# Where a broadcast write, a block of constants and twenty-seven small loads are issued, an earlier split of weights in four FFNs, and an attention mask added by TensorE

## The chip, the cores and the metric

One core of a Trainium2 chip runs the whole program. The metric is the device time of one execution in microseconds. TensorE (PE), VectorE (DVE), ScalarE (ACT), GpSimd (POOL) and SyncE (SP) run their own instruction streams and wait for each other by semaphores. DMAs are issued from two queues here, SP's (q1 in the trace) and ACT's (q10).

## The reference, cut to what matters

A model in float32 over 256 tokens of width 1024: first two layers, each FFN, mixer, FFN with modulation from `silu(c) @ ada_w`, then four layers, each mixer, cross attention to a memory, FFN.

```python
def first_block(...):
    c_act = silu(c)
    for l in range(2):
        mod = c_act @ ada_w[l] + ada_b[l]                  # nine vectors of 1024
        x = x + 0.5 * gt1 * swiglu(modulate(rmsnorm(x), sh1, sc1), ffn1_w_in[l], ffn1_w_out[l])
        # mixer: 8 heads of causal attention (here), a gated convolution, gated linear attention
        s = where(k_pos <= q_pos, q @ k.T * scale, -1e30); p = softmax(s)
        x = x + gt2 * mixed @ mix_w_out[l]
        x = x + 0.5 * gt3 * swiglu(modulate(rmsnorm(x), sh3, sc3), ffn2_w_in[l], ffn2_w_out[l])
def second_block(...):
    mem_n = rmsnorm(mem)
    for i in range(4):
        x = x + mixer_i(rmsnorm(x))          # i = 0 and 3: diff_attention, with rel_bias[:, bucket(q - k)]
        x = x + cross_attention(rmsnorm(x), mem_n)
        x = x + swiglu(rmsnorm(x), w_gu[i], w_down[i])
    return rmsnorm(x)
```

## The kernel before

**Weights.** Every weight matrix is cut into units of 128x2048 float32 (1 MB; 0.5 MB for an FFN's second matrix). SP streams them in one fixed order into four slots of `raw`; unit n of a slot may be loaded when unit n-1 has been split. ACT rounds a unit to `whi` (L710), DVE subtracts to get `wlo` (L1068), and PE multiplies hi by hi, hi by lo and lo by hi. `ahead(pos)` in ACT's and DVE's streams says where in the order of their work the next units are split: up to three units ahead, but no unit whose slot was last filled at or after `pos`. Splitting a unit waits until PE has used the slot's last one (`used`).

**FFN.** It has 11 steps. Step j multiplies the slots A and B (gate and up, `ab` or `ab_wide`), ACT and DVE form silu(a)*b, and `outs` multiplies it by the 0.5 MB units of the slots O0 and O1, while A and B of the next step have gone before. The order on PE is A0, B0, A1, B1, outs(0), A2, B2, outs(1), and so on. There are eight FFNs. The first four belong to the first block (`st.i` 0 to 3; the first also computes modulation in steps 0 to 9: two or four 1 MB units of `ada_w` a step, multiplied on DVE in `ada_pair`, L1169 and L1172). The last four are "deferred": PE starts on x times the gain while the norm's sum of squares is still under way, and the root is multiplied in afterwards (`st.defer`, L1262 to L1278). `rstd` is made by ACT at L769 and L771 after PE's sum (L1824), which PE does between A0 and B0.

**Start.** SP issues the first constants, the first rows, the memory, four units of `ada_w`, the tokens, and then `ada_w` and FFN units, the rest of the constants (0.83 MB) and the gate weights. ACT begins with 27 small loads (rows, convolution weights, bucket table, positions, lambdas), and then does silu of c and copies the transposed memory. PE transposes the rows and the memory, waits for all small loads (`rows_in`, `misc_in`), transposes them, and only then does the memory's norm sum (L1828), the bias line (a 33x384 product), the reductions of `ada_pair`, the tokens' transposes and two units of `ada_w` directly (L1771, 64 matmuls); then the norm of the first FFN.

**Bias rows.** DVE copies the bias line (8 heads x 384) into `raw` (slot 3), and SP writes it 128 times into a scratch tensor in HBM: 8 partitions, 1024 rows of 1536 bytes, 1.5 MB. The first use of slot 3 for weights waits for that write. The scratch tensor is read by the first `diff` stage, after the fourth FFN.

**Mixer of the first block.** Eight heads run in a loop of steps j (L1505 to L1541 on DVE, L1994 to L2029 on PE), interleaved with nine levels of the linear attention. In step j, DVE first updates the operands of level j (L1399, L1400), masks and takes the maxima of head j (L1514 to L1517), scales the probabilities of head j-1 (L1524, L1525) and keeps the level's blocks (L1424); PE does the scores of head j (L2002, L2003), transposes head j-2, multiplies the values of head j-3, and does level j (L1956), which waits for DVE's update.

Of the kernel before, what the change touches and what calls it, by code (L numbers as in the profile page):

```python
# [28 lines left out]
P = 128  # L29
D = 1024  # L30
KT = D // P
S = 256
# [175 lines left out]
def build(nc, a, out):  # L208

    ctx = ExitStack()  # L210
    with ctx:
# [69 lines left out]
        bias_line = raw[:, 3, 1408:1792]  # L281
# [112 lines left out]
        for l in range(DEPTH1):  # L394
# [12 lines left out]
                                masked=take("masked", 8), pairs=take("pairs", 4), tree=take("tree"),  # L407
# [181 lines left out]
        def _(sp):  # L589
# [34 lines left out]
            for st in stages:  # L624
                if st.kind == "prologue":
# [13 lines left out]
                    stream(1)  # L639
                    for u in range(6, 8):  # L640
                        ada(u)
                    stream(2)
                    load(q["const_rest"], con[:, N_FIRST:], c[:, N_FIRST:N_RESIDENT])
                    sp.wait_ge(q["pro_s"], 1)
                    load(q["const_rest"], gate_w[112:128, :, :], a["gla_gate_w"].rearrange("l r c -> r l c"))

                    sp.wait_ge(*PRO.at(0, "line"))
                    load(q["bias_out"], scratch.rearrange("r h c -> h r c"),
                         bias_line[0:8, :].rearrange("h (o c) -> h o c", o=1).broadcast_to([8, P, 384]))
                elif st.kind == "ffn":  # L650
                    stream(st.pos + 2)
                    if st.ada:
# [5 lines left out]
                        for j in range(STEPS - 1):  # L658
# [3 lines left out]
                            u += per[j]  # L662
                    stream(st.pos + 2 + 4 * (STEPS - 1) + 2)
# [38 lines left out]
        def _(act):  # L702
# [11 lines left out]
            def prologue(st):  # L714

# [13 lines left out]

                act.wait_ge(*PRO.at(0, "vec"))  # L730
                f(silu_c[:, :], col("c", 0, KT), ACT.Silu).then_inc(q["c_ready"], 1)
                for p in range(4):
                    act.wait_ge(q["tok_turned"], p + 1)
                    f(mem[:, 2 * p:2 * p + 2, :], ps[:, 4 + p, :], ACT.Copy).then_inc(q["tok_copied"], 1)
# [15 lines left out]
            def norm(st):  # L750
# [37 lines left out]
            def ffn(st):  # L788
                A, B, _, O1 = st.slots
                lo0 = STEPS * st.i  # L790
                for j in range(STEPS):
# [90 lines left out]
            def mix1(st):  # L882
# [174 lines left out]
        def _(dve):  # L1057
# [36 lines left out]
            def bias_and_lambda():  # L1094
                dve.wait_ge(q["misc_turned"], 2)
                pro("line", v.tensor_copy(bias_line[0:8, :], ps[0:8, 0, 0:384]))
# [6 lines left out]
            def prologue(st):  # L1103
                first_columns(st)
                other_columns(st)
# [1095 lines left out]
```

## Time and profile before

| | |
|---|---|
| three runs | 3074.69, 3080.16 and 3080.6 us; median 3080.16 |
| profiled execution | 3077.22 us, of which the span of the trace is 3075.4 us |
| mean granted TensorE clock | 0.960 of full |
| PE, PEld, DVE, ACT busy | 2855.6, 2694.5, 1956.7, 1370.3 us |
| chain that ended last | PE 81%, DVE 10%, ACT 3%, issue 3%, DMA 2% |
| HBM read, written | 528.10 MB, 2.62 MB |

Times in the trace count from the span's start. A busy PE is not PE at its peak: at the lower of its two clocks (0.50 in the rows, 1.2 GHz, against 1.00, 2.4 GHz) it is busy and half as fast. So both its idle time and the clock beside it have to be read.

### The profile page before, as it was taken

The numbers are of one execution on the slowest core, as the hardware profiler recorded it, in microseconds if no ns is written. First come the engines' busy times: TensorE is split into PE (matmuls) and PEld (weight loads), VectorE is DVE, ScalarE is ACT, GpSimd is POOL, SyncE is SP. The second block draws the span as 40 slices with busy tenths as digits, with TensorE's granted clock in tenths as the row PEclk, the third lists the DMA queues.
The fourth block names the chain that finished last, engine by engine and source line by source line (L and its number), as shares of the span: only waits on it lengthen the run. The fifth ranks groups of instructions, "written<-read, shape, count | busy, mean of one in ns | idle before, by whom it ended". The sixth has DMA issues, their size and how long they took to land.

```text
span 3075.4 us, 50735 instructions
## 1 busy us (share of the span) xinstructions
PE 2855.6 (93%) x21031; PEld 2694.5 (88%) x21031; DVE 1956.7 (64%) x2718; ACT 1370.3 (45%) x1640; POOL 0.7 (0%) x5
## 2 busy tenths in 40 slices
PE   6999879999998899969999978999989999979998
PEld 5999869999996899959899967989989899959897
DVE  5887767778768554555466674556655656555665
ACT  3335444343352444544444514454544544444443
POOL 0000000000000000000000000000000000000000
PEclk8999999999997999979999999999999999979999
DMA  8987418969852255615255613345654456513443
GB/s 239 317 276 243 136 42 280 299 217 301 294 161 82 79 193 187 212 55 165 94 191 181 205 55 111 123 165 181 202 165 137 140 188 204 193 51 128 158 171 109
DMA packets 458799, 533.02 MB, mean 173 GB/s; under 512 B 9879, under 2 KB 435081, under 8 KB 458633
## 3 DMA queue, kind: packets, MB, share of 16 engines
q1 hardware_dynamic: 457340, 530.11, 52.4%
q8 instruction: 109, 1.79, 0.2%
q10 hardware_dynamic: 1293, 0.65, 0.1%
q14 instruction: 57, 0.47, 0.0%
HBM read 528.10 MB, written 2.62 MB: 173 GB/s over the span
## 4 chain that ended last, share of the span: by engine, by line
PE 81%; DVE 10%; ACT 3%; issue 3%; DMA 2%; SPq 0%; ACTq 0%; DVEq 0%
PE ps L1887 14%; PE ps L1720 12%; PE ps L1872 11%; PE ps L2166 8%; PE ps L1873 5%; PE ps L1702 5%; PE ps L1704 5%; PE ps L1703 5%; PE ps L1750 2%; PE ps L1749 2%; PE ps L1748 2%; PE ps L1956 2%; DMA work<-in_ada_w 2%; PE ps L1927 2%; DVE work L1445 1%
## 5 line engine op out<-in xcount | busy, mean ns | idle before, releaser
L1068 DVE TENSOR_TENSOR wlo<-raw,whi 128x2048 fp32r<-128x2048 f32 (+1 forms) x514 | 977.1, 1920 | 475.2 <-ACT whi L710 474.9
L710 ACT ACTIVATE whi<-raw 128x2048 fp32r<-128x2048 f32 (+1 forms) x514 | 824.9, 1611 | 407.0 <-PE ps L1704 115.6
L1872 PE MATMUL ps<-parts_f,whi 128*128 128x512 f32 x1408 | 506.4, 403 | 9.0 <-issue 9.0
L1702 PE MATMUL ps<-hhi,whi 128*128 128x256 f32 x1360 | 390.3, 287 | 12.6 <-issue 10.0
L1873 PE MATMUL ps<-parts_f,wlo 128*128 128x256 f32 x1408 | 398.3, 283 | 0.0
L1703 PE MATMUL ps<-hlo,whi 128*128 128x256 f32 x1360 | 387.3, 285 | 0.0
L1704 PE MATMUL ps<-hhi,wlo 128*128 128x256 f32 x1360 | 387.3, 285 | 0.0
L1887 PE MATMUL ps<-ghi,whi 128*128 128x256 f32 x1280 | 362.4, 283 | 4.0 <-DVE wlo L1068 4.0
L1887 PE MATMUL ps<-glo,whi 128*128 128x256 f32 x1280 | 362.2, 283 | 0.0
L1887 PE MATMUL ps<-ghi,wlo 128*128 128x256 f32 x1280 | 362.1, 283 | 0.0
L1872 PEld LDWEIGHTS ps<-parts_f,whi 128*128 128x128 f32 x1408 | 267.7, 190 | 74.9 <-issue 10.2
L1702 PEld LDWEIGHTS ps<-hhi,whi 128*128 128x128 f32 x1360 | 263.9, 194 | 13.3 <-issue 13.0
L1873 PEld LDWEIGHTS ps<-parts_f,wlo 128*128 128x128 f32 x1408 | 269.1, 191 | 0.1
L1703 PEld LDWEIGHTS ps<-hlo,whi 128*128 128x128 f32 x1360 | 263.8, 194 | 0.0
L1704 PEld LDWEIGHTS ps<-hhi,wlo 128*128 128x128 f32 x1360 | 263.5, 194 | 0.0
L1887 PEld LDWEIGHTS ps<-ghi,whi 128*128 128x128 f32 x1280 | 245.4, 192 | 6.6 <-issue 4.5
L1720 PE MATMUL ps<-hhi,whi 128*128 128x256 f32 x1120 | 231.1, 288 | 17.0 <-DVE hlo L1233 16.2
L1887 PEld LDWEIGHTS ps<-ghi,wlo 128*128 128x128 f32 x1280 | 245.5, 192 | 0.0
L1887 PEld LDWEIGHTS ps<-glo,whi 128*128 128x128 f32 x1280 | 245.4, 192 | 0.0
L1720 PE MATMUL ps<-hhi,wlo 128*128 128x256 f32 x1120 | 227.3, 285 | 0.0
L1720 PE MATMUL ps<-hlo,whi 128*128 128x256 f32 x1120 | 227.2, 285 | 0.0
L1172 DVE SCALAR_TENSOR_TENSOR work<-work,silu_c 128x256 f32<-128x256 f32 x490 | 196.9, 480 | 0.0
(257 smaller groups left out, 4842.4 us busy)
## 6 DMA issues: line engine op xcount, KB each, us to landing
raw<-in_ffn_w_in SPq DMA_DIRECT2D x88, 1024.0 KB, 8.2
raw<-in_ffn_w_gu SPq DMA_DIRECT2D x88, 1024.0 KB, 5.0
work<-in_ada_w SPq DMA_DIRECT2D x72, 1024.0 KB, 8.7
raw<-in_ffn_w_out SPq DMA_DIRECT2D x88, 512.0 KB, 5.8
raw<-in_ffn_w_down SPq DMA_DIRECT2D x88, 512.0 KB, 5.7
raw<-in_ca_w_kv SPq DMA_DIRECT2D x32, 1024.0 KB, 5.8
raw<-in_mix_w_in SPq DMA_DIRECT2D x24, 1024.0 KB, 6.1
raw<-in_da_w_in SPq DMA_DIRECT2D x24, 1024.0 KB, 5.8
```

The lines of the kernel that those rows point to most:

```text
L710: f(whi[:, s, 0:size], raw[:, s, 0:size], ACT.Copy).then_inc(hi_done[s], 1)
L1068: tt(wlo[:, s, 0:size], raw[:, s, 0:size], whi[:, s, 0:size].bitcast(F32), ALU.subtract).then_inc(lo_done[s], 1)
L1172: m = stt(acc, w, silu_c[:, k:k + 1], acc, ALU.mult, ALU.add)
L1702: mm(dst, wh, xh, start=first, stop=False)
L1703: mm(dst, wh, xl, start=False, stop=False)
L1704: return mm(dst, wl, xh, start=False, stop=last)
L1720: o = mm(ps[:, slot, 256 * m:256 * m + 256], w[:, k, P * m:P * m + P], x_[:, k, :], start=k == 0 and i == 0 and m == 0, stop=k == KT - 1 a ...
L1748: mm(dst, xh[:, k, c], th[:, k, :], start=first, stop=False)
L1872: mm(ps[:, banks[m], :], th[:, k, c], parts_f[:, :, k, :], start=k == 0, stop=False)
L1873: o = mm(ps[:, banks[m], 0:S], tl[:, k, c], fhi[:, k, :], start=False, stop=k == KT - 1)
L1887: o = mm(dst, a_, b_[:, t, :], start=first and t == 0 and i == 0 and m % 2 == 0, stop=False, skip_group_check=True)
L2166: o = mm(ps[:, bank, 256 * m:256 * m + 256], w[:, k, P * m:P * m + P], x_[:, k, :], start=k == 0 and i == 0 and m == 0, stop=k == KT - 1 a ...
```

## The change

1. The write of the bias rows is issued by ACT in step 0 of the fourth FFN instead of by SP at the start. The line stands in `gate_w`, so that slot 3's first use waits for the transposes alone.
2. SP issues the large rest of the constants and the gate weights in step 5 of the first FFN.
3. ACT issues the 27 small loads in the memory's norm, behind silu of c, the memory's copies and its squares. PE does the memory's norm sum before it waits for them; DVE does `ada_pair(2, 1)` before the columns that they bring; PE's bias product stands behind `ada_pair(2, 1, 3)`.
4. In the deferred FFNs ACT and DVE also call `ahead(st.pos + 1)` in the norm, which splits A1; DVE waits for the root one instruction later.
5. In the first block's mixers PE adds the causal mask to the scores in PSUM (identity times mask, two float32 products a head), DVE takes the maxima from PSUM without a masking add, and ACT takes the exponential from PSUM.

```diff
@@ at the start: the line, slot 3, SP
-        bias_line = raw[:, 3, 1408:1792]
+        bias_line = gate_w[0:8, :, :].rearrange("p a b -> p (a b)")[:, 0:384]
...
-                                     (q["bias_out"], 16))[s])
+                                     (q["misc_turned"], 2))[s])
...
-                    stream(1)
                     for u in range(6, 8):
                         ada(u)
                     stream(2)
-                    load(q["const_rest"], con[:, N_FIRST:], c[:, N_FIRST:N_RESIDENT])
-                    sp.wait_ge(q["pro_s"], 1)
-                    load(q["const_rest"], gate_w[112:128, :, :], a["gla_gate_w"].rearrange("l r c -> r l c"))
-
-                    sp.wait_ge(*PRO.at(0, "line"))
-                    load(q["bias_out"], scratch.rearrange("r h c -> h r c"),
-                         bias_line[0:8, :].rearrange("h (o c) -> h o c", o=1).broadcast_to([8, P, 384]))
@@ SP, first FFN
+                            if (st.i, j) == (0, 5):
+                                c = a["constants"]
+                                load(q["const_rest"], con[:, N_FIRST:], c[:, N_FIRST:N_RESIDENT])
+                                sp.wait_ge(q["pro_s"], 1)
+                                load(q["const_rest"], gate_w[112:128, :, :], a["gla_gate_w"].rearrange("l r c -> r l c"))
@@ ACT, norm: the small loads, moved out of prologue() into small_loads()
                 if st.early or st.defer is not None:
                     ahead(st.pos)
+                if st.defer is not None:
+                    ahead(st.pos + 1)
+                if st.source == "mem":
+                    small_loads()
@@ ACT, ffn
+                    if (st.i, j) == (3, 0):
+                        act.wait_ge(*PRO.at(0, "line"))
+                        nc.scalar.dma_start(scratch.rearrange("r h c -> h r c"),
+                                            bias_line.rearrange("h (o c) -> h o c", o=1).broadcast_to([8, P, 384]))\
+                            .then_inc(q["bias_out"], 16)
@@ ACT, mix1
-                        s = m_s[:, j % 2, :]
-                        exp_rows(J, (s[:, 0:P], s[:, P:384]), (s[:, 0:P], s[:, P:384]), stat[:, j % 2, 0:2],
+                        if J > 1:
+                            act.wait_ge(q["turned_mm"], J - 1)
+                        d, s = ps[:, (4, 0)[j % 2], :], m_s[:, j % 2, :]
+                        exp_rows(J, (d[:, 0:P], d[:, P:384]), (s[:, 0:P], s[:, P:384]), stat[:, j % 2, 0:2],
@@ DVE, prologue
                 first_columns(st)
+                ada_pair(2, 1)
                 other_columns(st)
-                ada_pair(2, 1)
                 bias_and_lambda()
@@ DVE, deferred norm and ffn
                     ahead(st.pos)
+                    ahead(st.pos + 1)
                     return
...
-                        if j == 0:
-                            dve.wait_ge(q["norm_rs"], st.late.i + 1)
...
                         dve.wait_ge(read[A], st.reads[A] + j + 1)
+                        if j == 0:
+                            dve.wait_ge(q["norm_rs"], st.late.i + 1)
                         tt(silu_a, silu_a, root, ALU.mult).then_inc(q["ffn_a"], 1)
@@ DVE, mix1
-                            dve.wait_ge(q["turned_mm"], J - 1)
-                        s = m_s[:, j % 2, :]
-                        tt(s, ps[:, (4, 0)[j % 2], 0:384], causal, ALU.add).then_inc(q["masked"], 1)
-                        dve.wait_ge(q["masked"], st.masked + j + 1)
-                        v.tensor_reduce(stat[:, j % 2, 0:1], s[:, 0:P], AX.X, ALU.max, negate=True)
-                        v.tensor_reduce(stat[:, j % 2, 1:2], s[:, P:384], AX.X, ALU.max, negate=True)\
+                            dve.wait_ge(q["exped"], J - 1)
+                        d = ps[:, (4, 0)[j % 2], :]
+                        v.tensor_reduce(stat[:, j % 2, 0:1], d[:, 0:P], AX.X, ALU.max, negate=True)
+                        v.tensor_reduce(stat[:, j % 2, 1:2], d[:, P:384], AX.X, ALU.max, negate=True)\
@@ PE, prologue and start: the waits for the small loads and the transposes of them come into start()
                 turn_tokens(0, tok_mem)
+
+            def start(st):
                 n_rows = sum(2 if r in ("q_norm", "k_norm", "gla_out_norm") else 1 for r in ROWS) - len(FIRST_ROWS)
                 pe.wait_ge(q["rows_in"], 16 * n_rows)
...
-
-            def start(st):
-                pe.wait_ge(*PRO.at(0, "cols"))
-                mm(ps[0:8, 0, 0:384], bias_cols[0:BUCKETS + 1, :], bucket[0:BUCKETS + 1, :], start=True,
-                   stop=True).then_inc(q["misc_turned"], 1)
                 ada_pair(0, 0, 3)
                 pe.wait_ge(q["token_in"], 16)
                 turn_tokens(1, tok_x)
                 ada_pair(2, 1, 3)
+                pe.wait_ge(*PRO.at(0, "cols"))
+                mm(ps[0:8, 0, 0:384], bias_cols[0:BUCKETS + 1, :], bucket[0:BUCKETS + 1, :], start=True,
+                   stop=True).then_inc(q["misc_turned"], 1)
@@ PE, mix1
-                        mm(d[:, 0:P], mq[rows_, tile, 0:P], mk[rows_, tile, 0:P], start=True, stop=True)
-                        mm(d[:, P:384], mq[rows_, tile, P:S], mk[rows_, tile, :], start=True, stop=True)\
-                            .then_inc(q["scores_mm"], 1)
+                        mm(d[:, 0:P], mq[rows_, tile, 0:P], mk[rows_, tile, 0:P], start=True, stop=False)
+                        mm(d[:, 0:P], ident, causal[:, 0:P], start=False, stop=True)
+                        mm(d[:, P:384], mq[rows_, tile, P:S], mk[rows_, tile, :], start=True, stop=False)
+                        mm(d[:, P:384], ident, causal[:, P:384], start=False, stop=True).then_inc(q["scores_mm"], 1)
```

## Rows read from the trace of the kernel before

**Rows 1.** The page: the chain that ended last, by engine.

```profile
PE 81%; DVE 10%; ACT 3%; issue 3%; DMA 2%; SPq 0%; ACTq 0%; DVEq 0%
```

**Rows 2.** Windows at the start: engines busy, then PEclk, DMA share, GB/s.

```profile
24.00:44.00 20.00, 20.00 (x106) 17.77 (x104) 16.83 (x51) 8.72 (x18) 0.00 (x0) 0.83 1.06 349
...
57.00:68.00 11.00, 8.33 (x55) 8.07 (x54) 5.86 (x10) 5.78 (x8) 0.00 (x0) 0.84 0.46 53
```

**Rows 3.** Timeline of ACT and its queue: start, duration, operation (first and last of 27 small loads).

```profile
0.73 0.42 ACTq L717 DMA_DIRECT2D raw<-in_mix_norm  x1
...
12.74 0.74 ACTq L717 DMA_DIRECT2D work<-in_da_lk  x1
...
18.28 2.19 ACT L762 ACTIVATE work<-raw 128x512 f32<-128x512 f32 x4
```

**Rows 4.** Timeline of PE to the first FFN; in brackets idle before it.

```profile
7.62 3.67 PE L1693 MATMUL ps<-con,raw 128*128 128x128 f32 x16 [3.20 <-DMA raw<-in_mem]
...
23.70 0.64 PE L1693 MATMUL ps<-con,raw 31*128 31x31 f32 x5 [8.62 <-DMA work<-in_da_lk]
24.27 6.68 PE L1828 MATMUL ps<-work,con 128*128 128x256 f32 x16
...
55.47 0.47 PE L1720 MATMUL ps<-hhi,whi 128*128 128x256 f32 x2 [2.15 <-DVE hlo L1233]
```

**Rows 5.** Timelines of SP, ACT and PE around the bias write.

```profile
39.42 0.81 SPq L593 DMA_DIRECT2D bias_rows<-raw  x1
50.28 17.13 SPq L593 DMA_DIRECT2D raw<-in_ffn_w_in  x2
...
76.39 1.91 ACT L710 ACTIVATE whi<-raw 128x2048 fp32r<-128x2048 f32 x1 [12.45 <-DMA raw<-in_ffn_w_in]
...
80.72 0.55 PE L1702 MATMUL ps<-hhi,whi 128*128 128x256 f32 x1 [8.78 <-issue]
```

**Rows 6.** DMA queues in 13:19: packets, MB, share of 16 engines.

```profile
q1 hardware_dynamic: 1329, 1.33, 70.6%
q10 hardware_dynamic: 872, 0.51, 31.9%
```

**Rows 7.** Timelines of ACT and DVE in the fourth FFN, steps 0 to 2.

```profile
1065.65 3.79 ACT L710 ACTIVATE whi<-raw 128x2048 fp32r<-128x2048 f32 x3
...
1087.52 0.60 ACT L807 ACTIVATE work<-ps 128x512 f32<-128x512 f32 x1 [1.30 <-PE ps L1704]
...
1067.58 4.57 DVE L1068 TENSOR_TENSOR wlo<-raw,whi 128x2048 fp32r<-128x2048 f32 x3 [2.50 <-ACT whi L710]
```

**Rows 8.** Waits of PE in 300:700 and 700:1000; timelines of PE (second mixer), DVE (first).

```profile
PE ps L1956 <- DVE work L1400: 8.3, 6, 2.2
...
PE ps L1956 <- DVE work L1400: 4.1, 4, 2.0
...
996.91 0.63 PE L2002 MATMUL ps<-work 64*128 64x128 f32 x2
997.34 1.06 PE L2003 MATMUL ps<-work 64*128 64x256 f32 x2
...
1000.63 2.24 PE L1956 MATMUL ps<-work 64*128 64x128 f32 x16
...
388.70 0.55 DVE L1514 TENSOR_TENSOR work<-ps,con 128x384 f32<-128x384 f32 x1
```

**Rows 9.** Waits of PE; then its timeline and DVE's in the first deferred FFN.

```profile
PE ps L1872 <- issue: 9.0, 4, 2.3
...
1524.30 0.47 PE L1872 MATMUL ps<-parts_f,whi 128*128 128x512 f32 x1 [2.25 <-issue]
...
1521.91 2.29 DVE L1068 TENSOR_TENSOR wlo<-raw,whi 128x2048 fp32r<-128x2048 f32 x1 [2.50 <-ACT whi L710]
```

**Rows 10.** Windows there: columns as in rows 2.

```profile
1510.00:1515.00 5.00, 5.00 (x30) 4.34 (x29) 4.20 (x8) 1.43 (x3) 0.00 (x0) 1.00 0.46 184
1525.00:1528.50 3.50, 3.50 (x14) 2.97 (x13) 1.09 (x2) 2.29 (x2) 0.00 (x0) 0.55 0.88 288
```

More of the change, by code:

```diff
@@ L406, in build @@
             stages.append(Stage(kind="mix1", l=l, units=units, last=units[-1], gn=take("gn", 5), heads=take("heads", 8),
-                                masked=take("masked", 8), pairs=take("pairs", 4), tree=take("tree"),
+                                pairs=take("pairs", 4), tree=take("tree"),
                                 rope=take("rope", 4)))
@@ L714, in prologue, with small_loads @@
             def prologue(st):
+                act.wait_ge(*PRO.at(0, "vec"))
+                f(silu_c[:, :], col("c", 0, KT), ACT.Silu).then_inc(q["c_ready"], 1)
+                for p in range(4):
+                    act.wait_ge(q["tok_turned"], p + 1)
+                    f(mem[:, 2 * p:2 * p + 2, :], ps[:, 4 + p, :], ACT.Copy).then_inc(q["tok_copied"], 1)
+            def small_loads():
                 def load(semaphore, dst, src):
@@ L728, in prologue @@
                          a[name].partition_broadcast(P).rearrange("p a b -> p (a b)"))
[L730 to L734, printed above, removed]
             def rope_tables():
@@ L1095, in bias_and_lambda @@
                 dve.wait_ge(q["misc_turned"], 2)
-                pro("line", v.tensor_copy(bias_line[0:8, :], ps[0:8, 0, 0:384]))
+                pro("line", v.tensor_copy(bias_line, ps[0:8, 0, 0:384]))
                 pro("cols_s", ts(lam[:, 14:16], col("q_norm", 0, 2), 0.125, None, ALU.mult))
@@ L1494, in mix1 @@
                 rope(3)
-                causal = const("causal")
                 gate_ready = 4 * l + 4
@@ L1987, in mix1 @@
                 pe.wait_ge(q["rope_done"], st.rope + 4)
+                causal = const("causal")
                 def part(h):
@@ L1997, in mix1 @@
                         rows_, tile = part(j)
-                        if st.masked + j > 1:
-                            pe.wait_ge(q["masked"], st.masked + j - 1)
+                        if st.heads + j > 1:
+                            pe.wait_ge(q["exped"], st.heads + j - 1)
                         d = ps[:, (4, 0)[j % 2], :]
-                        mm(d[:, 0:P], mq[rows_, tile, 0:P], mk[rows_, tile, 0:P], start=True, stop=True)
-                        mm(d[:, P:384], mq[rows_, tile, P:S], mk[rows_, tile, :], start=True, stop=True)\
-                            .then_inc(q["scores_mm"], 1)
+                        mm(d[:, 0:P], mq[rows_, tile, 0:P], mk[rows_, tile, 0:P], start=True, stop=False)
+                        mm(d[:, 0:P], ident, causal[:, 0:P], start=False, stop=True)
+                        mm(d[:, P:384], mq[rows_, tile, P:S], mk[rows_, tile, :], start=True, stop=False)
+                        mm(d[:, P:384], ident, causal[:, P:384], start=False, stop=True).then_inc(q["scores_mm"], 1)
                     if 2 <= j <= 9:
@@ L2061, in diff @@
                     if j < 8:
-                        pe.wait_ge(q["masked"], st.masked + j - 1)
+                        if st.masked + j > 1:
+                            pe.wait_ge(q["masked"], st.masked + j - 1)
                         for c in range(2):
```

## The prediction

> **What bounds the kernel now.** I read the page first. PE makes up 81% of the chain that ended last and DMA 2% [rows 1], so in most places only PE's time counts; the places where PE stands still or runs at its lower clock are what the change can reach. I then read PE's waits, the timelines of the four stretches that the diff touches, and windows over them.
>
> At the start the DMA engines are full until 44 us (share 1.06, 349 GB/s), then only the bias write is left: share 0.46 and 53 GB/s [rows 2]. PE waits 8.62 us for the last small load, which was issued at 12.74 and is used at 23.70, and the first FFN begins at 55.47 [rows 3, 4]. SP issued the bias write at 39.42. The load of A1, issued at 50.28 on the same queue, lands only at 76.39, and PE stands still 8.78 us before A1's product [rows 5]. In the four deferred FFNs PE waits 9.0 us in all, 2.25 us each, between B0 and A1 [rows 9]. In the two mixers DVE and PE take turns.
>
> **Part 1: small loads behind silu of c.** They take ACT's queue from 0.73 to 13.48, so 12.75 us for 27. Now ACT does silu, the four copies, a table load and four squares first. The memory's transposes end at 7.62 + 3.67 = 11.29; the last copy adds 0.5, the table load 1.28 and the squares 2.2 [rows 3, 4]: the issue starts at 15.3 and ends at 28.05. The last load starts its issue at 27.3. Before, the last one needed 10.9 us from issue to use (12.74 to 23.70); that gives 38.2. From below it lands at once, 28.1. The engines remain full in between, as they were then, so I take 37. After that load PE had 31.8 us of work and waits to the first FFN, of which 6.6 us were the memory's norm sum (L1828), now done ahead [rows 4]. The rest, 25.2 us, is serial as before: DVE's work behind the bias line is in the same order. First FFN: 37 + 25.2 = 62.2, against 55.5. Term: +6.7 us, from -2.2 to +7.9. Silu comes early, and with it the first two `ada_pair`, but nothing on this path waits for them.
>
> **Part 2: the bias write leaves the start.** A1's load has free engines, lands some 5 us after its issue, and PE goes on after B0. The stall of 8.78 us goes [rows 5]. What is late next is DVE's chain of the step (splits of A1, B1, O0, O1 and two `ada_pair`), which begins with A1's split and moves forward as a whole. I take -8.7; from -4 (if the four `ada_w` units, 4 MB at 349 GB/s or 12 us, become the wait) to -11 (with a stretch at the lower clock gained back).
>
> **Part 3: large constants in the first FFN.** 0.83 MB at 349 GB/s are 2.4 us of all engines. At the start they lay behind everything that PE waited for; in step 5 they lie between weights that are due some 10 us later. +0.3, from 0 to +2.4. The same 3 MB of weights and 2 MB of `ada_w` a step hide it.
>
> **Part 4: the bias write in the fourth FFN.** 53 GB/s are 34.5 rows of 1536 bytes a microsecond. The share of 0.46 means that some 8 of 16 engines carry it [rows 2], 128 rows each at 0.232 us. A 1 MB weight unit has 64 rows of 1 KB for each engine, at 349/16 GB/s or 0.047 us each, so 3 us. On ACT's queue the write no longer stands ahead of the weights in one line; but while both queues had work, at 13 to 19 us, their packets passed at similar rates, 1329 and 872 [rows 6]. I read that as turn by turn on each engine. Then a weight unit needs 64 x (0.232 + 0.047) = 17.9 us on the shared engines. The write is issued after `ghi` of step 0, at 1065.7, which by the 0.81 us of that issue [rows 5] also puts ACT's next splits back (B1's is just in time: +0.5). B2's load can start when B1 is split, 1067.58 + 2.2 [rows 7] plus the 0.8; it flows from about 1072.6 and lands at 1090.5. A2's product ends at 1087.5 (ACT's silu follows it [rows 7]); to be ready then, B2 must land 4.2 us earlier (1.9 for hi, 2.3 for lo), at 1083.3. It is 7.2 us late. Behind it 16 rows of O0 and O1 and the next A, of which 28 rows still alternate, land at about 1106; PE, now 7.2 us later, wanted that A at 1102: 4.1 us more. Lower clock after two such stalls: I add 2. Sum +14. From both sides: 0 if weights pass first, +22 if the write's 29.7 us pass first.
>
> The Trainium skill ("DMA: Bandwidth & Descriptors", section Queues, rings and completion order) says that each engine goes round-robin between its rows of queues, a whole packet of about 9 to 17 descriptors at a time. Working with its figures, an estimate, one turn of the write would last 2 to 4 us and B2 land up to that much later, for a sum of about +16 to +18; the records in this trace look finer than that.
>
> **Part 5: A1 split early in the deferred FFNs.** Before, DVE splits A1 from 1521.91 to 1524.1, PE waits 2.25 us for it [rows 9] and then runs at clock 0.55 for 3.5 us, doing 14 matmuls where 6 a microsecond are normal (30 in 5): 3.5 - 14/6 = 1.2 us lost [rows 10]. Now ACT splits A1 when A0's product ends at about 1515.4, before it makes `rstd`; the root comes 0.9 us later, and DVE's lo of A1 ends at 1519.7, before PE ends B0 at 1522.05. Late next is B1: its slot is free at 1522.05, then a copy 0.6, two DVE operations 1.3, `ghi` 0.6, hi 1.9, lo 2.3, with gaps 1528.9; PE, at full clock, would want it at 1527.6: a new wait of 1.3. For each FFN -(2.25 + 1.2 - 1.3) = -2.15, for four -8.6. Bounds: -3.8 (the clock falls again) to -13.8 (no new wait).
>
> **Part 6: mask by PE.** Removed: 16 DVE additions of 0.55 us [rows 8]. Added: 32 float32 products of identity and mask. The scores' 128-column pair takes 0.43 us from start to start at the lower clock [rows 8], the 256-column pair twice that: 1.28 us a head at the lower clock, about 0.65 at the full one. If all of it hid nothing, +20.8 at the lower clock; if PE had slack everywhere and DVE always bound, -8.8. PE waits for DVE before a level, 6 times in the first mixer (8.3 us) and 4 times in the second (4.1 us), up to 2.2 us [rows 8], and there the products fit in. But head 0 stands ahead of level 0, in steps 4 and 6 DVE waits for ACT's `hhi` behind PE's scores and transposes, and in the second mixer level 6 follows PE's own work without a gap [rows 8]. Counting along the chain: first mixer 1.3 (head 0) + 0.7 (level 3) + 2 x 0.65 - 2 x 0.6 (two steps that DVE bounds) = +2.1; second 1.3 + 0.15 + 0.9 + 1.3 + 1.3 + 0.65 - 2 x 0.6 = +4.4. I take +6, range -4 to +12 as most of the bounds can't hold in all steps.
>
> **Sum.** 6.7 - 8.7 + 0.3 + 14 - 8.6 + 6 = +9.7. The profiled execution took 3077.2 us (span 3075.4 and 1.8 around it): 3086.9. The median of the runs shown, 3080.2, is 2.9 higher, but they spread over 6; I forecast 3087.
>
> **Rivals.**
> (a) *The write in the fourth FFN does not hold the weights.* Then part 4 is +0.5 and the sum -3.8: 3073 with the rest as worked out. This is the case that ends on the other side. It decides once B2 lands before 1083.3, so if a 1 MB unit passes in under 10.7 us beside the write. For it: an alternating packet share of 40 to 60 [rows 6] was read with small packets, and DMA there is under half used. Against it: 0.232 us a row is five times a weight row.
> (b) *PE has room for the mask*, because its extra work also lifts its clock: part 6 is -4, sum -0.3, 3077: no change.
> (c) *Small loads land soon after issue* (31): part 1 is +0.7, sum +3.7, 3081: no change.
> (d) *The early split gains little* (-3.8) since the wait only moves to B1: sum +14.5, 3092.
> The early split could also do nothing if A1 were not landed by then, but it was issued before B0's split ended, 15 us ahead.
>
> **How the numbers follow.** Likeliest, 0.42: all terms near what I took, 3087, own range 3079 to 3097. Rival (a) 0.25, (b) 0.10, (c) 0.10, (d) 0.13. About 0.2% or 6.2 us is what a measurement of this kernel can tell from no change. Slower by more: 0.30 of the first, 0.11 of (d), 0.03 of (c), together 0.44. Same: 0.12 + 0.05 of (a) + 0.06 of (b) + 0.07 of (c) + 0.02 of (d) = 0.32. Faster: 0.20 of (a) and 0.04 of (b) = 0.24. The range reaches down to 3068 (rival (a) with a cheaper mask) and up to 3102 (part 4 at its upper bound).
>
> **What the profile after would show.** Part 1: PE's wait for the last small load ends near 37 and the first FFN begins near 62; near 55 it is wrong. Part 2: no wait of PE before A1's product. Part 4: in the fourth FFN DMA share high at low GB/s for some 35 us, and PE waits of 5 us or more before B2's product; none, and (a) holds. Part 5: no wait at L1872 after B0, a shorter one at B1's product, no clock near 0.5 there. Part 6: each mixer loop 2 to 4 us longer. Wrong I would be most easily in part 4, the largest term, and read from the least direct rows.

## The result, and the profile after

The changed kernel takes 3092.64 us (median of 5, 3089.2 to 3094.02), the kernel before 3080.6 on the same chip (5 runs, 3074.69 to 3083.43): ratio 1.0036, interval 1.0024 to 1.0048. It is slower, by 12 us in the medians. The profiled execution of the changed kernel took 3093.57 us with a span of 3091.8, 16.4 more than the span shown of before.

The page of the changed kernel: the chain that ended last, by engine.

```profile
PE 81%; DVE 10%; DMA 3%; ACT 3%; issue 2%; SPq 1%; ACTq 0%; DVEq 0%
```

Against [rows 1], DMA went from 2% to 3%. That is all that a summary shows of it. So I set each matmul of one trace beside the same matmul of the other and read how much later it begins. PE reaches the first FFN 12 us later, but A1's product of that FFN only 2 us later (82.70 against 80.72), and is 5 to 6 behind from 179 to 300 us, 10 at 429, 6 at 1053, 25 at 1100 and 16 at the end. Where the large steps come from is read below. One trace is not exact about the start: the six kernels whose start is the changed kernel's (it, and experiments 1, 2, 3, 7 and 8) reach the first FFN between 63.6 and 68.4 us and A1's product between 79.7 and 84.4, so a step of a few us there says nothing by itself.

**The start.** Timeline of PE to the first FFN.

```profile
13.89 6.43 PE L1835 MATMUL ps<-work,con 128*128 128x256 f32 x16 [2.63 <-ACT work L760]
26.89 0.73 PE L1700 MATMUL ps<-con,raw 104*128 104x104 f32 x3 [6.57 <-DMA raw<-in_ada_b]
36.31 0.65 PE L1700 MATMUL ps<-con,raw 31*128 31x31 f32 x5 [8.69 <-DMA work<-in_da_lk]
...
45.07 13.81 PE L1778 MATMUL ps<-silu_c,work 128*128 128x1 f32 x64
58.74 6.18 PE L1835 MATMUL ps<-work,con 128*128 128x256 f32 x16
...
67.85 0.76 PE L1727 MATMUL ps<-hhi,whi 128*128 128x256 f32 x2 [2.14 <-DVE hlo L1243]
```

ACT's queue in the same stretch (start, duration): first and last small load.

```profile
13.22 0.39 ACTq L721 DMA_DIRECT2D raw<-in_mix_norm  x1
...
25.43 0.74 ACTq L721 DMA_DIRECT2D work<-in_da_lk  x1
```

Windows there: busy time of PE, PEld, DVE, ACT, POOL, then PEclk, DMA share, GB/s.

```profile
20.00:40.00 20.00, 4.74 (x25) 4.11 (x24) 7.26 (x25) 0.89 (x2) 0.00 (x0) 0.57 1.03 319
40.00:60.00 20.00, 20.00 (x88) 18.53 (x87) 13.88 (x38) 10.31 (x18) 0.00 (x0) 0.50 0.18 57
60.00:80.00 20.00, 17.55 (x96) 16.38 (x96) 12.51 (x21) 10.54 (x15) 0.00 (x0) 0.73 0.28 83
```

The last small load is used at 36.31 instead of 23.70 [rows 4]. PE did the memory's norm sum ahead and then has nothing: it stands still for 6.57 and 8.69 us, and from 40 to 60 it is busy without a pause at clock 0.50, the lower of its two levels (1.2 GHz). Busy in full, with half the speed: the busy column alone would have shown nothing wrong. From the last load to the first FFN it took 31.5 us. The wait of 8.78 us for A1 [rows 5] is gone: between 76 and 100 us PE waits 0.3 us in all.

**The fourth FFN.** Timelines of ACT and its queue, DVE, SP and PE.

```profile
1071.24 0.31 ACTq L828 DMA_DIRECT2D bias_rows<-gate_w  x1
...
1076.71 1.91 ACT L707 ACTIVATE whi<-raw 128x2048 fp32r<-128x2048 f32 x1
1105.38 2.86 ACT L707 ACTIVATE whi<-raw 128x2048 fp32r<-128x2048 f32 x2 [26.76 <-DMA raw<-in_ffn_w_in]
...
1107.32 3.43 DVE L1077 TENSOR_TENSOR wlo<-raw,whi 128x2048 fp32r<-128x2048 f32 x2 [24.44 <-ACT whi L707]
...
1077.21 11.11 SPq L593 DMA_DIRECT2D raw<-in_ffn_w_out  x2
1088.40 21.66 SPq L593 DMA_DIRECT2D raw<-in_ffn_w_in  x2
...
1109.72 0.55 PE L1709 MATMUL ps<-hhi,whi 128*128 128x256 f32 x1 [16.11 <-issue]
```

Windows there (columns as above).

```profile
1072.00:1100.00 28.00, 21.61 (x179) 21.31 (x178) 8.06 (x6) 5.97 (x5) 0.00 (x0) 0.96 0.69 141
1100.00:1112.00 12.00, 2.28 (x11) 2.31 (x12) 4.68 (x4) 6.57 (x7) 0.00 (x0) 0.50 0.54 149
```

The DMA queues in three windows, 1076:1082, 1084:1088 and 1098:1104 (packets, MB, share of 16 engines; q10 is ACT's queue with the write, q1 SP's with the weights), and of the first the landing time of the weights issued in it.

```profile
q10 hardware_dynamic: 194, 0.30, 43.8%
q1 hardware_dynamic: 522, 0.53, 28.9%
raw<-in_ffn_w_in SPq DMA_DIRECT2D x1, 1024.0 KB, 29.3
...
q10 hardware_dynamic: 129, 0.20, 43.7%
...
q10 hardware_dynamic: 193, 0.30, 42.0%
q1 hardware_dynamic: 192, 0.20, 9.2%
```

The write's rows pass from 1073 to 1104 at an unvarying 32 a microsecond, whatever the weights do. B2, issued at 1076, first moves its half on the engines that don't carry the write (522 packets by 1082); then no weight packet at all (1084 to 1088); then weight rows and write rows one for one (192 and 193), and B2 lands with the end of the write, 29.3 us after its issue. PE stands still for 16.1 us and goes on at clock 0.50. This one stall is larger than the whole loss.

**The deferred FFNs and the mixers.** Waits of PE in the changed kernel (total, times, longest); then, of 300:1010 alone, the wait before the levels.

```profile
PE ps L1709 <- issue: 16.5, 2, 16.1
PE ps L1894 <- DVE wlo L1077: 6.6, 3, 3.0
PE ps L1879 <- issue: 5.5, 4, 1.4
...
PE ps L1963 <- DVE work L1410: 7.6, 7, 1.3
```

Against [rows 9], L1879 (L1872 before) waits 1.4 us an FFN instead of 2.25; it is now B1's product and not A1's. In the mixers the waits for DVE before a level [rows 8] became fewer and shorter: 7.6 us in 7 waits, longest 1.3, where the kernel before has 13.7 us in 11 over the same stretch, longest 2.2.

### The profile page after: what moved, and what is told of

Read it like the earlier page. It is cut to its first block, busy times and chain, and to the rows that moved or that the text cites. A ratio compares the mean times of both kernels' runs of the same rounds, so it can differ in the third digit from the quotient of the medians.

```text
span 3091.8 us, 50863 instructions
## 1 busy us (share of the span) xinstructions
PE 2869.4 (93%) x21095; PEld 2704.0 (87%) x21095; DVE 1948.5 (63%) x2702; ACT 1368.1 (44%) x1640; POOL 0.7 (0%) x5
## 4 chain that ended last, share of the span: by engine, by line
PE 81%; DVE 10%; DMA 3%; ACT 3%; issue 2%; SPq 1%; ACTq 0%; DVEq 0%
PE ps L1894 14%; PE ps L1727 12%; PE ps L1879 11%; PE ps L2177 8%; PE ps L1880 5%; PE ps L1709 5%; PE ps L1711 5%; PE ps L1710 5%; PE ps L1757 2%; PE ps L1755 2%; PE ps L1756 2%; DMA work<-in_ada_w 2%; PE ps L1963 2%; PE ps L1934 2%; DVE wlo L1077 1%
## 5 line engine op out<-in xcount | busy, mean ns | idle before, releaser
L1879 PE MATMUL ps<-parts_f,whi 128*128 128x512 f32 x1408 | 500.4, 399 | 5.5 <-issue 5.5
L1879 PEld LDWEIGHTS ps<-parts_f,whi 128*128 128x128 f32 x1408 | 264.7, 188 | 70.1 <-issue 6.7
```

Source lines behind the costliest of these rows:

```text
L1879: mm(ps[:, banks[m], :], th[:, k, c], parts_f[:, :, k, :], start=k == 0, stop=False)
```

## The experiments

All were timed beside the kernel before (3080.22, 3080.45 and 3081.42 us in three sets); "later" and "earlier" are again from the same matmul in two traces.

### 1. The bias write in the second mixer

```diff
-                    if (st.i, j) == (3, 0):          # ACT, fourth FFN: the write
...
                 log_exp_tables()
+                if st.l == 1:
+                    act.wait_ge(*PRO.at(0, "line"))
+                    nc.scalar.dma_start(scratch.rearrange("r h c -> h r c"), ...)
                 for j in range(8 + 3):
```

> The changed kernel, but ACT issues the bias write ahead of the second mixer's head loop instead of in step 0 of the fourth FFN. Theory: the write holds the weights of the fourth FFN on the engines it uses, and that costs the 18.4 us by which PE falls back there; the DMA engines are idle in the mixer loop (share 0.00), so the 31 us of the write fit in: 18 us less than the changed kernel, about 3074, 0.2% below the kernel before. Rival: PE falls back in the fourth FFN for another reason (ACT issuing, or the early order of the loads); then it stays near 3092.

3073.74 us (9 runs), ratio 0.9977 (0.9965 to 0.9988): 18.9 less than the changed kernel. A window over the fourth FFN, and from the DMA view of 953:985 the landing of a weight unit that is issued beside the write in the mixer:

```profile
1065.00:1100.00 35.00, 35.00 (x293) 34.91 (x292) 20.07 (x16) 19.45 (x17) 0.00 (x0) 1.00 0.62 211
```

```profile
raw<-in_ffn_w_in SPq DMA_DIRECT2D x1, 1024.0 KB, 27.9
```

PE is busy for all 35 us at clock 1.00. The write still holds a unit of weights for 27.9 us, but in a mixer nobody waits for it. Beside the changed kernel's trace this one is 4.3 us earlier at 1053 us, ahead of the fourth FFN, and 23.0 at 1115: 18.7 us are gained there. So the write in the fourth FFN cost some 19 us, and the place is what made it cost.

The order of the rows is the same here as in the FFN. DMA queues in 964:972 and 974:984 (the write was issued at 952.77, the held unit at 959.05):

```profile
q10 hardware_dynamic: 259, 0.40, 44.2%
...
q10 hardware_dynamic: 311, 0.48, 42.3%
q1 hardware_dynamic: 309, 0.32, 8.9%
```

For 8 us, and 32 rows of the write on each of its engines, not one row of weights passed; then they went one for one. In both places the change came some 17 to 19 us into the write.

### 2 and 3. The write in eight pieces, and in two halves

```diff
-                    if (st.i, j) == (3, 0):
+                    if st.i == 3 and j < 8:          # the halves: j in (0, 4), 64 rows of each head
-                        nc.scalar.dma_start(scratch.rearrange("r h c -> h r c"), ... [8, P, 384]
+                        nc.scalar.dma_start(scratch[16 * j:16 * j + 16].rearrange("r h c -> h r c"), ... [8, 16, 384]
...
```

SP's wait before it reads the scratch tensor counts all the pieces.

> The changed kernel, with the bias write cut into eight DMAs of 16 of the 128 copies, one in each of the steps 0 to 7 of the fourth FFN. Same bytes, same queue, same FFN. Theory (the weights of the engines that the write uses come one row after each row of the write, or not at all while more than about half of a long write is still ahead of them): 16 rows an engine are over in 4 us, less than the 10 us of slack of a unit: no wait of PE, 17 us less than the changed kernel, about 3075. Rival (the 31 us of the write cost PE the same wherever they are spread in the FFN): 16 us of waits in eight pieces, about 3092.

> The changed kernel, with the bias write cut into two DMAs of 64 copies, in the steps 0 and 4 of the fourth FFN. In the changed kernel the weights' rows on the write's engines came from 1090 on only, half way through the write, and from then one for one with it. Theory A (only so much of a DMA stands ready on each engine, and the second half of the write is taken up before the weights behind it): with 64 rows the weights come one for one from the first, B2 lands some 16 us after its issue instead of 29 and PE waits about 4 us a half: 8 us in all, half of now, about 3084. Theory B (the write passes first, the weights after it, whatever its length): each half costs its 15 us less some 13 of slack: 2 to 4 us in all, about 3079.

Eight pieces: 3070.12 us (8 runs), ratio 0.9969 (0.9956 to 0.9983), 22.5 less than the changed kernel. Two halves: 3073.88 (10 runs), ratio 0.9984 (0.9974 to 0.9994). Not all of the 22.5 us belong to the write: beside the changed kernel's trace the eight pieces are 1.8 us earlier at 1053 us and 20.4 at 1115, so 18.6 are gained in the fourth FFN, as in experiment 1, and another 3.9 in two stages far behind it, at about 1820 and 2700 us, which the edit doesn't touch. The halves gain 15.7 in the FFN, 3 less. A window of the eight pieces; then of the halves ACT's wait for B2, and the landing time of the weights issued in 1068:1083.

```profile
1062.00:1200.00 138.00, 138.00 (x1151) 137.91 (x1150) 70.81 (x67) 63.99 (x57) 0.00 (x0) 1.00 0.59 194
```

```profile
1086.56 2.86 ACT L707 ACTIVATE whi<-raw 128x2048 fp32r<-128x2048 f32 x2 [13.36 <-DMA raw<-in_ffn_w_in]
```

```profile
raw<-in_ffn_w_in SPq DMA_DIRECT2D x2, 1024.0 KB, 13.7
```

The same 1.5 MB through the same queue in the same FFN cost PE no wait if they come 4 us at a time: a piece holds a unit for less than the lead that the weights have. A half (some 15 us) holds B2 about until its own end, and PE waits 2.7 us once; the second half costs no wait. So it is the length of one write beside the lead of the loads, not its bytes. In the trace of the halves the weights' rows on the shared engines come at the very end of the write: they followed it, and did not go one for one. That is theory B's picture, though its time (3079) was 5 us too long.

### 4 and 5. The old start, and the loads alone

```diff
             def prologue(st):
+                small_loads()
                 act.wait_ge(*PRO.at(0, "vec"))
...
-                if st.source == "mem":
-                    small_loads()
```

The "old start" also takes back the order of PE and DVE (transposes of the rows in PE's prologue, the bias product first in `start`, `ada_pair(2, 1)` behind `other_columns`); the write stays in the fourth FFN.

> The changed kernel with the small loads first on ACT's queue again and PE's and DVE's order of the start as before; the bias write and the large constants stay where the change put them. Theory: the late small loads cost 12.4 us at the start of the first FFN: 12 us less than the changed kernel, about 3080, and the first FFN begins near 55. Rival: part of the delay comes back inside the first FFN, whose first two steps wait for ada_w units: 5 to 8 us less, about 3086.

> The changed kernel with one thing of the start undone: the 27 small loads stand first on ACT's queue again, while PE's and DVE's new order (the memory's norm sum and the second ada_pair ahead of them) stays. Theory: the small loads' landing alone sets the start, near 24 us instead of 36, and the memory's sum is off that path: the first FFN begins at 50 to 52, 4 us earlier than in the kernel before, and the run takes 16 us less than the changed kernel, about 3076. Rival: the first FFN is then held by the ada_w units (8 MB before its second step), and all beyond the old start (12 us) is lost again: 3080.

Old start: 3078.52 us (10 runs), ratio 0.9999 (0.9990 to 1.0009): 14.1 less than the changed kernel. Loads alone: 3080.92 (10 runs), ratio 1.0004 (0.9995 to 1.0014), 11.7 less. PE in the old start, then with the loads alone:

```profile
23.73 0.65 PE L1699 MATMUL ps<-con,raw 31*128 31x31 f32 x5 [8.71 <-DMA work<-in_da_lk]
...
33.66 10.28 PE L1777 MATMUL ps<-silu_c,work 128*128 128x1 f32 x64
...
52.38 0.48 PE L1726 MATMUL ps<-hhi,whi 128*128 128x256 f32 x2 [2.14 <-DVE hlo L1242]
```

```profile
18.84 5.66 PE L1834 MATMUL ps<-work,con 128*128 128x256 f32 x16 [7.57 <-ACT work L761]
...
32.40 13.24 PE L1777 MATMUL ps<-silu_c,work 128*128 128x1 f32 x64
...
54.41 0.77 PE L1726 MATMUL ps<-hhi,whi 128*128 128x256 f32 x2 [2.14 <-DVE hlo L1242]
```

The old start reaches the first FFN at 52.38, the loads alone at 54.41, the changed kernel at 67.85. I had expected a gain from the memory's norm sum before the small loads; there is none: PE waits 7.57 us for ACT's squares, and then the 64 products take 13.24 us instead of 10.28. The rival's time (3080) was right; that the `ada_w` units are what takes the gain back isn't shown. The two runs reach A1's product 12.0 and 11.5 us before the kernel before did, and the four runs of experiments 9 to 12, with the same old start, 9.6 to 12.9. That is what taking the bias write out of the start is worth at this place; experiment 11 shows that the constants have no part in it. By 300 us 8 to 10 of it are left in all six.

### 6. PE kept busy while it waits

```diff
+                for _ in range(26):                  # 36 more before the wait for misc_in
+                    turn(ps[:, 3, 0:P], ident)
                 pe.wait_ge(q["rows_in"], 16 * n_rows)
```

It adds 62 transposes of the identity whose results nobody reads.

> The changed kernel, where PE also does 26 and 36 transposes of the identity into a free bank while it waits for the small loads. They add work that nobody uses and leave the result as it is. Theory: of the 12.4 us by which the first FFN begins later, 6 come from the lower TensorE clock (0.50 from 27 to 74 us) after PE stood still for 16 us; with PE busy the clock stays up, the work from the last small load to the first FFN takes 25 us instead of 31.5, and the run is 5 to 6 us shorter, about 3087. Rival: the clock falls in the stretch of one-column matmuls whatever PE did before: no change, 3092.

3088.2 us (6 runs), ratio 1.0024 (1.0011 to 1.0037), 4.4 less than the changed kernel. Windows:

```profile
20.00:40.00 20.00, 13.04 (x95) 12.47 (x94) 7.36 (x25) 0.89 (x2) 0.00 (x0) 0.83 1.01 318
40.00:60.00 20.00, 18.80 (x90) 17.31 (x88) 17.26 (x43) 11.65 (x21) 0.00 (x0) 0.66 0.20 65
```

With useless work before the last load (used at 35.91, hardly sooner than 36.31) the clock behind it is 0.66 instead of 0.50, and the first FFN begins at 60.95 instead of 67.85; A1's product at 77.10 instead of 82.70. The other five traces with the new start have clocks of 0.50 to 0.62 there, the first FFN at 63.6 to 68.4 and A1's product at 79.7 to 84.4, so the filler is worth 3 to 7 us by the traces. In the medians it is 4.4 us, with intervals that overlap. So of the 14.1 us of the new start a few, 4 as the best guess, are the clock, and the rest the late loads. The Trainium skill ("TensorE: Matmul & The Clock Gate", section HAM oscillation) tells of the same thing in a loop that waits for its DMAs: the waits throttle PE, and the work behind each of them starts cold. The two traces agree, with 0.50 behind waits of 6.57 and 8.69 us and 0.66 where the filler left 4.6 and 2.4 of them.

### 7. The mask by DVE again

```diff
-                        mm(d[:, 0:P], ident, causal[:, 0:P], start=False, stop=True)
...
+                        tt(s, ps[:, (4, 0)[j % 2], 0:384], const("causal"), ALU.add).then_inc(q["masked"], 1)
```

> The changed kernel with the mask added by DVE again. Between the traces the first mixer lost about 3 us and the second gained about 5. Theory A (extra PE work lifts the clock sooner in the second mixer): undoing it changes the sum by +2 (-1 to +4), about 3094. Theory B (as forecast: +6.5 us along the chain of DVE and PE, and the second mixer's gain is chance of the clock): 4 to 6 us less, about 3087.

3093.96 us (7 runs), ratio 1.0036 (1.0024 to 1.0049): the changed kernel's own ratio. The mask by PE costs nothing measurable here. Waits of PE in 300:1010:

```profile
PE ps L1963 <- DVE work L1408: 10.9, 9, 2.0
...
PE ps L1963 <- DVE work L1398: 5.0, 2, 2.5
```

With the addition on DVE, PE waits 10.9 us before the levels instead of 7.6, and 5.0 more for L1398, of which the changed kernel (there L1400) has 0.7 left. That fits products that lie in time in which PE waited.

### 8. A1 split late again

```diff
-                if st.defer is not None:              # ACT; on DVE the same call
-                    ahead(st.pos + 1)
```

> The changed kernel without the early split of A1 in the four deferred FFNs (DVE's later wait for the root stays). Theory: the wait of 2.25 us before A1 and the stretch at the lower clock come back four times, while the wait of 1.4 us before B1 goes: 12 us more than the changed kernel (-3.0 a FFN between the traces), about 3104. Rival (only the difference of the waits counts, 0.9 us each, the clock being chance): 3 to 4 us more, 3096.

3097.21 us (4 runs), ratio 1.0059 (1.0039 to 1.0080): the early split is worth 4.6 us in the medians, with intervals that overlap. Without it: waits of PE, then windows 1532:1552 and 1816:1826; in the third fence the same windows of the changed kernel.

```profile
PE ps L1876 <- issue: 9.0, 4, 2.3
```

```profile
1532.00:1552.00 20.00, 17.77 (x97) 15.36 (x97) 9.83 (x14) 9.19 (x12) 0.00 (x0) 0.92 0.36 128
1816.00:1826.00 10.00, 6.64 (x57) 6.51 (x58) 8.63 (x18) 0.00 (x0) 0.00 (x0) 1.00 0.00 0
```

```profile
1532.00:1552.00 20.00, 19.13 (x111) 16.50 (x110) 11.81 (x15) 11.49 (x15) 0.00 (x0) 1.00 0.37 128
1816.00:1826.00 10.00, 7.45 (x45) 7.29 (x45) 6.96 (x14) 0.00 (x0) 0.00 (x0) 0.72 0.00 0
```

At the first deferred FFN the clock stays at 1.00, and behind each of the four PE is 2.4 or 2.5 us earlier (within the first for a moment 4.0). That makes 9.8 us, more than the 8.6 forecast. The rival's time (3096) was nearer than the theory's, but its reason, that only the waits differ, isn't: without the early split the clock there is 0.92. They don't all reach the end: the lead of the first is gone by 1825, where the products of the linear attention's levels (L1963; L1960 in the file without the early split) are done at clock 0.72 where the run without the early split has 1.00. The other three leads are kept but for 1.1 us: 3.0, 5.4 and 6.8 us earlier behind the second, third and fourth FFN. Whether the early split is what lowers that clock, experiment 12 can tell.

### 9 to 12. Both repairs, and three parts priced on top

The old start (experiment 4) with the write in eight pieces (experiment 2); then the same with DVE's mask (the diff of 7), with the constants at the end of SP's prologue (below), and without the early split (the diff of 8).

```diff
                     stream(2)
+                    load(q["const_rest"], con[:, N_FIRST:], c[:, N_FIRST:N_RESIDENT])
...
-                            if (st.i, j) == (0, 5):
```

> The two repairs together: the small loads stand first on ACT's queue with the old order of PE and DVE at the start, and the bias write goes out in eight pieces of 16 rows in steps 0 to 7 of the fourth FFN. Theory: the two costs lie in different places and add: the start is worth 14.1 us against the changed kernel (3092.6 to 3078.5), the pieces are worth 22.5 (to 3070.1), so 3056, ratio 0.992; with the clock giving a little back 3054 to 3062. Rival: a gain at the start is given back before the third FFN (PE meets the same weights' loads sooner), as much of it was where the loads alone were moved: 3064 to 3070.

> As the run with both repairs, but DVE adds the mask again and PE multiplies only queries and keys. Prices the mask by PE where no other part of the change disturbs the mixers. As predicted (+6 for the mask by PE): 6 faster than the run with both repairs. By the run that undid the mask alone (3093.96 against 3092.64): the same within 3. Rival, PE has room: 4 slower than the run with both repairs, and it would show in the second mixer.

> As the run with both repairs, but the large constants and the gate's rows are loaded at the end of SP's prologue again, behind the weights of unit 2. In all versions so far PE lost 2 to 4 us between 101 and 376 us against the kernel before, and step 5 of the first FFN lies at 179. Theory: the constants hold the weights behind them there: then this run gains 2 to 3 us, and the loss between 101 and 376 is gone. Rival: the loss is the lead of the start that the weights' loads take back whatever stands between them: no difference within 2 us, and the constants delay no product at the start either.

> As the run with both repairs, but A1 is split late in the deferred FFNs, as before. Prices the early split a second time. As predicted: 8.6 slower than the run with both repairs. As the run that undid it alone measured (3097.2 against 3092.6): 4.6 slower. Rival, the wait only moved to B1: 2 slower or less.

| kernel | us (5 runs each) | ratio, interval |
|---|---|---|
| both repairs | 3062.63 | 0.9943, 0.9929 to 0.9956 |
| and mask by DVE | 3065.05 | 0.9950, 0.9936 to 0.9963 |
| and constants at the start | 3061.17 | 0.9933, 0.9919 to 0.9946 |
| and no early split | 3066.91 | 0.9957, 0.9943 to 0.9970 |

The chain of both repairs, by engine:

```profile
PE 85%; DVE 8%; ACT 3%; issue 2%; DMA 1%; SPq 0%; ACTq 0%; DVEq 0%
```

Both repairs together beat the kernel before by 0.57% (18.8 us) and the changed kernel by 30 us. The sum of the two differences of medians would have been 36.6, so the theory's 3056 was missed, and 3062.63 lies between it and the rival's 3064. But the rival's reason, that something is given back, doesn't show: beside the changed kernel's trace both repairs are 14.1 us earlier at 300 us, 13.9 at 1053 and 32.5 at 1115, so the start's 14 and the write's 18.6 are there in full, and 30.9 at the end. What is missing is mostly the 3.9 by which experiment 2's 22.5 exceed the 18.6 gained at the write, and 1.6 lost between 1200 and 1520.

Window 375:430, in the first mixer, with both repairs, and (second fence) with DVE's mask as well:

```profile
375.00:430.00 55.00, 46.22 (x294) 32.91 (x294) 38.14 (x118) 21.48 (x53) 0.00 (x0) 0.88 0.00 1
```

```profile
375.00:430.00 55.00, 47.02 (x242) 32.24 (x240) 38.49 (x114) 20.48 (x51) 0.00 (x0) 0.65 0.00 1
```

The mask by PE is worth 2.4 us in the medians, with intervals that overlap; in the traces PE is 5.6 us earlier behind the second mixer, of which 2.3 are left at the end. In these runs it goes with a clock of 0.88 instead of 0.65 in the same stretch; the kernel before, with DVE's mask, has 0.81 there, so the clock of a mixer hangs on more than the mask. The constants are worth nothing in either place (1.5 us, overlapping intervals). The loss against the kernel before between 101 and 376 us stays (2.9 us with the constants at the start, 3.2 without) and so does that between 300 and 429 (4.8 and 4.6): they are not its cause.

The early split is worth 4.3 us in the medians, as in experiment 8. The traces tell more. Behind each of the four FFNs the kernel with it gains 2.3 to 2.5 us again. The kernel without it, however, was 2.8 us ahead before the first deferred FFN, 2.3 of them gained between 1115 and 1520 where both kernels do the same. And the products that ran at 0.72 in experiment 8's comparison do so in both kernels here. Window 1785:1795, with and (second line) without the early split:

```profile
1785.00:1795.00 10.00, 7.45 (x44) 7.29 (x44) 6.93 (x14) 0.00 (x0) 0.00 (x0) 0.72 0.00 0
...
1785.00:1795.00 10.00, 7.45 (x44) 7.29 (x44) 6.46 (x12) 0.00 (x0) 0.00 (x0) 0.73 0.00 0
```

So that clock isn't the price of the early split. What sets it is open.

## Why the prediction was right, and where it was not

The forecast of 3087 with a range of 3068 to 3102 and "slower" as the likeliest held: 3092.64. The range's upper end has a slip: part 4 at its bound of 22 instead of 14 makes 3095 of 3087, not 3102; the measured time lies below either. Part by part, what was forecast and what the runs showed:

| part | forecast | measured |
|---|---|---|
| 1 small loads behind silu | +6.7 | +14.1 (experiment 4) |
| 2 bias write leaves the start | -8.7 | -10 to -13 at A1, -8 to -10 at 300 us (traces of experiments 4, 5, 9 to 12) |
| 3 constants | +0.3 | 0 within 2 (experiment 11) |
| 4 bias write in the fourth FFN | +14 | +18.6 and +18.7 (traces of experiments 1, 2 in that FFN) |
| 5 early split | -8.6 | -9.5 and -9.8 at the four FFNs, -4.6 and -4.3 in the medians (experiments 8, 12) |
| 6 mask by PE | +6 | -1.3, -2.4 (experiments 7, 10) |

With -10 for part 2 and the medians for part 5 the measured parts add to 14.1 - 10 + 0 + 18.7 - 4.5 - 1.9 = +16.4, more than the 12 of the medians and as much as between the two traces; to the tenth that is chance, since medians and traces are mixed and no part is known to better than 1 or 2 us. That the forecast of +9.7 came near the 12 was luck in part, because its errors stood on both sides: parts 1, 4 and 5 together were 16 too low, part 6 some 8 too high.

**Part 1**: the mechanism and the first number were right (last load used at 36.31, taken as 37). The term that was mis-sized is "25.2 us, serial as before": it took 31.5, since the 25.2 were read where PE had a clock of 0.83 from 24 to 44 us [rows 2] and it is 0.50 from 40 to 60 here. A serial stretch was carried over with its duration, but behind new idle time. In the other five traces with the new start the stretch took 27.5 to 32.0 us, and 25.0 in experiment 6, where PE was kept busy in the waits. So the idle time is worth 2.5 to 7 us of it, which is most of the 7.4 by which the part was too low.

**Part 2**: no wait before A1 is left, as forecast; the gain at A1 (10 to 13) was about the bound of 11 or above it, of which up to 4 are given back by 300 us.

**Part 4**: the place, the mechanism (the write holds the weights on the 8 shared engines) and rival (a)'s refutation were right. Mis-sized was the term "64 x (0.232 + 0.047) = 17.9 us", turn by turn: it took 29.3 us, and the upper bound named, the write's whole time passing first, was nearly what came. The reading behind it, that queues pass at similar rates in 13:19 [rows 6], was of small packets on ACT's queue (0.51 MB in 872); in the fourth FFN one for one held only behind about 1090 us, the last 14 of the write's 31 us, and in the mixer of experiment 1 from about 972, the last 13 of its 32. The sentence on the Trainium skill's packet-wise round-robin came to +16 to +18 and was nearer than mine, but its rule doesn't show in the packets either: for 8 us, 32 of the write's rows an engine, not one weight packet passed (experiment 1), and then they alternated row by row. The second stall forecast (4.1 us at the next A) didn't come, since the write was over when B2 landed.

**Part 5**: the new wait (1.3 forecast, 1.4 measured, four times) and the removed one with its clock were right for each FFN, and so was the gain: 2.3 to 2.5 us, where 2.15 was forecast. What the forecast lacks is that only half of the four gains shows in the medians. Part of it went at a clock of 0.72 in experiment 8, and in experiment 12 the kernel without the early split had got 2.3 us elsewhere; neither is shown to come from the early split, and with 4 and 5 runs the medians themselves are uncertain by some 3 us.

**Part 6**: counted along the chain in both mixers, it gave +6; rival (b), that PE has room (-4), was nearer. The step that failed is "head 0 stands ahead of level 0, in steps 4 and 6 DVE waits for ACT's `hhi` behind PE's scores", each taken at its full price: PE's waits for DVE before a level fell from 13.7 to 7.6 us over both mixers. The mixers' time alone doesn't settle it. They did change (+4 in the first, -4 in the second, changed kernel against before), but they change likewise, even more, with DVE's mask (experiment 7), so this is not the mask.

## What to carry to other kernels

Cut a slow write into pieces that are shorter than the lead of the loads which share its DMA engines, or put it where no load is due: here the same bytes cost 19 us in the FFN as one DMA, 3 as two and no wait at all as eight. A serial stretch moved behind a wait must be priced at the clock that it will meet there; read PEclk beside the busy time, since a busy PE at 0.50 looks like a healthy one. And a difference of two kernels' times is not yet the price of the edit: set the two traces side by side and see where it arises. Here 22.5 us were 18.6 at the write and 3.9 in stages that the edit didn't touch, and of 9.8 us gained at four FFNs the medians showed 4.6.

## What the runs showed of the hardware that I had not expected

- One long write held a weight unit of another queue on the shared engines until the write's own end: 29.3 us for 1 MB (5 us without it), in the mixer 27.9, and 13.7 with a write half as long. On the shared engines no weight row passed in the first 17 to 19 us of the long write (in 964:972 of experiment 1, 259 rows of the write and none of the weights), and later they went one for one. Why the order changes is open; the runs only show that the write's own rate hardly moved (32 rows of 1536 bytes a microsecond, 50 GB/s).
- The write uses some 8 of 16 engines (share 0.44 when alone). By the Trainium skill ("DMA: Bandwidth & Descriptors", section Why a DMA increments its semaphore by 16 and not by 1) the number of engines follows from the slowest dimension of the access pattern, which here is the 8 heads; the share agrees. A write with its outermost dimension a multiple of 16 wasn't tried.
- Idle time at the start lowered the clock for a long while: with 6.57 and 8.69 us of waiting the 20 us from 40 to 60 ran busy at 0.50 (0.50 to 0.62 in the other five traces with this start); with filler the clock was 0.66, and the way from the last load to the first FFN took 25.0 us instead of 27.5 to 32.0.
- The clock of one and the same stretch of small products differed between kernels whose edits lie elsewhere: 0.72, 0.73 and 1.00 for the levels behind the first deferred FFN. What sets it is open.
